# The last two rounds of a mixture of experts: a gated sum on VectorE instead of identity products on TensorE

## The reference, cut to what matters

```python
x  = layer_norm(ALPHA * x + g1 * mix, ln1_g, ln1_b)
h2 = x * (1.0 + sc2) + sh2
y2 = sum over e of comb[t, e] * (silu(h2 @ w_gate[e]) * (h2 @ w_up[e])) @ w_down[e]   # 16 experts
x  = layer_norm(ALPHA * x + g2 * y2, ln2_g, ln2_b)
```

## Time and profile before

| | us |
|---|---|
| median of 3 runs | 480.96 (479.89 to 482.44) |
| the profiled execution | 481.61 |
| its span, first to last instruction | 479.8 |
| TensorE busy | 433.2 (90%) |
| VectorE busy | 244.1 (51%) |
| ScalarE busy | 120.8 (25%) |
| TensorE's mean granted clock | 0.975 of full |

### The profile page before, as it was taken

How to read it: one execution, slowest core, us unless ns; L and a number is a source line. 1 busy time by engine, 2 the same in 40 slices (tenths; PEclk the granted TensorE clock), 3 DMA queues, 4 the chain that set the end, 5 groups by cost and what they waited for, 6 DMA issues and landing times.

```text
span 479.8 us, 6399 instructions
## 1 busy us (share of the span) xinstructions
PE 433.2 (90%) x2352; PEld 229.2 (48%) x2352; DVE 244.1 (51%) x457; ACT 120.8 (25%) x229; POOL 39.9 (8%) x41
## 2 busy tenths in 40 slices
PE   0878999999999988899999999999999999899850
PEld 0434555555444443784554355554455554355220
DVE  4562725737864687971132353344554445333666
ACT  3300186285311032360120011121111111021143
POOL 2000043054000000390000000000000000000000
PEclk9999999999999995999999999999999999999995
DMA  8999994408999883808999999999999999999303
GB/s 300 387 387 381 305 387 146 161 0 198 386 387 404 333 290 104 308 2 314 376 396 397 370 359 395 396 391 392 397 394 391 393 396 394 392 392 404 127 2 132
DMA packets 65363, 149.50 MB, mean 312 GB/s; under 512 B 3624, under 2 KB 4504, under 8 KB 64936
## 3 DMA queue, kind: packets, MB, share of 16 engines
q1 hardware_dynamic: 63776, 143.33, 80.7%
q10 hardware_dynamic: 1384, 5.48, 2.9%
q0 software_dynamic: 160, 0.10, 0.5%
HBM read 147.30 MB, written 1.60 MB: 310 GB/s over the span
## 4 chain that ended last, share of the span: by engine, by line
PE 74%; DMA 9%; DVE 5%; issue 4%; ACT 4%; SPq 3%; DVEq 0%; ACTq 0%
PE PS L1746 19%; PE PS L1541 11%; PE PS L1623 9%; PE PS L1786 8%; PE PS L1752 6%; DMA ring<-in_w_ada 5%; PE PS L1820 4%; DMA ring<-in_ex_w_gate 4%; PE PS L1703 3%; SPq L379 3%; PE PS L1479 3%; PE PS L1524 2%; PE PS L1793 1%; PE PS L1828 1%; PE PS L1766 1%
## 5 line engine op out<-in xcount | busy, mean ns | idle before, releaser
L1746 PE MATMUL PS<-ring,xs 128*64 128x256 f32 x896 | 102.9, 382 | 1.3 <-DMA ring<-in_ex_w_gate 1.2
L1746 PEld LDWEIGHTS PS<-ring,xs 128*64 128x64 f32 x896 | 61.9, 137 | 37.7 <-issue 9.1
L1541 PE MATMUL PS<-hT,ring 128*128 128x388 f32 x192 | 65.3, 491 | 2.9 <-DMA ring<-in_w_in 2.1
L1786 PE MATMUL PS<-ring,hTs 128*64 128x512 f32 x224 | 51.1, 598 | 2.2 <-ACT hTs L675 1.4
L1541 PEld LDWEIGHTS PS<-hT,ring 128*128 128x128 f32 x192 | 36.1, 190 | 30.4 <-DMA ring<-in_w_in 2.4
L1288 DVE SCALAR_TENSOR_TENSOR y<-PS,comb,y 128x1024 f32<-128x1024 f32 x39 | 49.8, 1277 | 0.3 <-PE PS L1828 0.3
L1786 PEld LDWEIGHTS PS<-ring,hTs 128*64 128x64 f32 x224 | 14.8, 136 | 31.0 <-issue 30.9
L1274 DVE TENSOR_TENSOR yl<-PS,yh 128x512 fp32r<-128x512 f32 x12 | 8.3, 692 | 41.0 <-ACT yh L693 41.0
L1752 PE MATMUL PS<-ring,xs 128*128 128x512 f32 x64 | 28.0, 592 | 0.0
L693 ACT CAST yh<-PS 128x512 fp32r<-128x512 f32 x12 | 7.0, 587 | 81.3 <-PE PS L1786 62.9
L1479 PE MATMUL PS<-ring,cond 128*32 128x512 f32 x192 | 24.9, 656 | 2.1 <-DMA ring<-in_w_ada 2.1
(11 more groups left out here) (270 smaller groups left out, 554.8 us busy)
## 6 DMA issues: line engine op xcount, KB each, us to landing
ring<-in_ex_w_gate SPq DMA_DIRECT2D x16, 2048.0 KB, 13.4
ring<-in_ex_w_up SPq DMA_DIRECT2D x16, 2048.0 KB, 13.5
ring<-in_ex_w_down SPq DMA_DIRECT2D x16, 2048.0 KB, 14.2
ring<-in_w_ada SPq DMA_DIRECT2D x12, 2048.0 KB, 16.1
ring<-in_w_in SPq DMA_DIRECT2D x3, 2048.0 KB, 20.4
ring<-in_w_out SPq DMA_DIRECT2D x2, 2048.0 KB, 18.4
rows<-row_scratch ACTq DMA_DIRECT2D x3, 1024.0 KB, 7.6
xn<-in_x_sample SPq DMA_DIRECT2D x2, 512.0 KB, 6.7
```

Of the source, the lines that this page charges most:

```text
L1541: mm = pe.matmul(PS[:, w % 4, 0:W], wt[:, k, (w % 4) * P:(w % 4 + 1) * P], hT[:, k, :], start=(k == 0), stop=(k == KD - 1))
L1746: mm = pe.matmul(PS[HALF * h:HALF * (h + 1), j, 0:FE // 2], x[:, k, 0:HALF], w[:, k, h * (FE // 2):(h + 1) * (FE // 2)], start=(k == 0), s ...
L1786: mm = pe.matmul(PS[HALF * h:HALF * (h + 1), yb, :], x, w[:, f, h * 512:(h + 1) * 512], start=(f == 0), stop=(f == KF - 1))
```

## The change

- `add_sum` is gone. TensorE's end is now combine(14, 0), combine(14, 1), combine(15, 0), combine(15, 1), combine(14, 2), combine(15, 2), and every combine of expert 14 starts its banks anew.
- A new step `gated(i)` on VectorE multiplies `y12[:, i, :]` (the sum of the first 14 experts) by `g2` and adds `ALPHA * xn`, in place, once `gather(13, i)` is done. `gated(0)` stands before `hidden(15)`, `gated(1)` after `gather(13, 1)`, `gated(2)` after `choose(15)` and before `y_low(15)`.
- `z(i)` multiplies the banks by `g2` into a new tile `ztmp` (in the ring slot of expert 15's gate weights), then adds `y12[:, i, :]`; this second instruction also gives the row's sum by `accum_out`, so ScalarE's pass over the row for the sum (L751) is gone.
- `choose` is cut in two: `row_weights(e)` (the look-up) and `choose(e)` (`selT`). `row_weights(14)` and `choose(14)` move from round 14 to the end of round 13, after gather(12, 2); `row_weights(15)` and gather(13, 2) move before `y_low(14)`; `choose(15)` stands after `y_low(14)`.
- ScalarE runs a square root on a scratch column after `hid_out(14)`, and `hid_out(15)` moves before `y_out(14)`. Its order in the tail is moments(0), root, moments(1), root, moments(2), root.

```diff
+        ztmp = at("ztmp", base + (3 * LAST - 1) % SLOTS * RB, [P, NT, D])
...
-                hid_out(e)
+                if e < LAST:
+                    hid_out(e)
+                if e == LAST - 1:
+                    act.activation(small[:, 4:5], cst[:, 0:1], ACT.Sqrt)
+                    hid_out(LAST)
...
                 act.wait_ge(s["z_done"], i + 1)
                 need(act, "mom_sq", i)
-                act.activation(gsum[:, :], y12[:, i, :], ACT.Copy, accum_out=stat[:, i, 0:1]).then_inc(s["mom_sum"], 1)
-                act.wait_ge(s["mom_sum"], i + 1)
                 act.activation(stat[:, i, 1:2], stat[:, i, 0:1], ACT.Copy, scale=-1.0 / D).then_inc(s["mom_mean"], 1)
...
-                moments(0)
-                moments(1)
-                root(2 * NT)
-                moments(2)
-                root(2 * NT + 1)
-                root(2 * NT + 2)
+                for i in range(NT):
+                    moments(i)
+                    root(2 * NT + i)
...
+            def gated(i):
+
+                m = y12[:, i, :]
                 if i == 0:
                     dve.wait_ge(s["g2_sb"], 4)
+                dve.wait_ge(s["acc_done"], NT * (LAST - 2) + i + 1)
+                link(dve.tensor_tensor(m, m, g2r[:, 1 if i else 0, :], ALU.mult))
+                dve.scalar_tensor_tensor(out=m, in0=xn[:, i, :], scalar=ALPHA, in1=m, op0=ALU.mult, op1=ALU.add)\
+                    .then_inc(s["gated"], 1)
+
+            def z(i):
+
+                m, b = y12[:, i, :], c_banks(LAST, i)
                 dve.wait_ge(s["p_ps"], i + 1)
-                link(dve.tensor_tensor(m, PS[:, b:b + 2, :].rearrange("p a n -> p (a n)"), g2r[:, 1 if i else 0, :],
-                                       ALU.mult))
-                dve.scalar_tensor_tensor(out=m, in0=xn[:, i, :], scalar=ALPHA, in1=m, op0=ALU.mult, op1=ALU.add)\
-                    .then_inc(s["z_done"], 1)
+                link(dve.tensor_tensor(ztmp[:, i, :], PS[:, b:b + 2, :].rearrange("p a n -> p (a n)"),
+                                       g2r[:, 1 if i else 0, :], ALU.mult))
+                dve.wait_ge(s["gated"], i + 1)
+                dve.scalar_tensor_tensor(out=m, in0=ztmp[:, i, :], scalar=1.0, in1=m, op0=ALU.mult, op1=ALU.add,
+                                         accum_out=stat[:, i, 0:1]).then_inc(s["z_done"], 1)
...
                 if e:
                     gather(e - 1, 0)
+                if e == LAST - 1:
+                    gated(0)
                 hidden(e + 1)
-                choose(e)
+                if e < LAST - 1:
+                    choose(e)
                 if e:
                     gather(e - 1, 1)
+                if e == LAST - 1:
+                    gated(1)
+                    row_weights(LAST)
+                    gather(e - 1, 2)
                 y_low(e)
-                if e == LAST - 1:
-                    choose(LAST)
-                if e:
+                if 0 < e < LAST - 1:
                     gather(e - 1, 2)
+                if e == LAST - 2:
+                    row_weights(LAST - 1)
+                    choose(LAST - 1)
+
+            choose(LAST)
+            gated(2)
             y_low(LAST)
...
             for i in range(NT - 1):
                 combine(LAST - 1, i)
-                add_sum(i)
             for i in range(NT - 1):
                 combine(LAST, i)
-            add_sum(NT - 1)
             combine(LAST - 1, NT - 1)
             combine(LAST, NT - 1)
```

More of the change, by code:

```diff
@@ L250, in build @@
             "gelu_done yr_done maps_ps maps_sb fold_done z_ps z_sb f_ps yf_sb row_ps row_sb mix_ps x1n "
-            "g1_out g1_in mod2_out sc2_in sh2_in "
+            "gated g1_out g1_in mod2_out sc2_in sh2_in "
             "x1_done h2_done mod2_done h2hi h2lo h2T_ps h2T_sb lg_ps assign_done rank_ps route_done "
@@ L258, in build @@
             "g2_ps g2_sb fin_done wrow_ps wrow_sb wsum_a wsum_b p_ps z_done "
-            "out_done var_done root_done mom_sum mom_mean mom_sq").split()}
+            "out_done var_done root_done mom_mean mom_sq").split()}
         pos_in = [sem(f"pos_in{i}") for i in range(NT - 1)]
@@ L1232, in choose, with rows_of, row_weights @@
                 need(dve, "c_ps", NT * (e - 1))
+                def rows_of(q):
+                    dve.tensor_scalar(seltmp[:, :], Prow[:, 0, :], io[:, q, e:e + 1], None, ALU.is_equal)\
+                        .then_inc(s["selA2"], 1)
+                    dve.wait_ge(s["selA2"], e + 1)
+                    dve.scalar_tensor_tensor(out=selT[e % 2][:, :], in0=Prow[:, 1, :], scalar=io[:, q, e:e + 1],
+                                             in1=seltmp[:, :], op0=ALU.is_equal, op1=ALU.add).then_inc(s["selT_done"], 1)
+                fork(dve, counts[e], lambda: rows_of(0), lambda: rows_of(1))
+            def row_weights(e):
                 if e == LAST - 1:
                     dve.wait_ge(s["wrow_sb"], 2)
+                need(dve, "selT_done", e)
                 def weights_of(q):
@@ L1245, in weights_of @@
                     dve.wait_ge(s["wsum_b"], e - LAST + 2)
[L1247 to L1256, removed]
+                fork(dve, counts[e], lambda: weights_of(0), lambda: weights_of(1))
             def y_low(e):
@@ L1289, in gather @@
                                              op0=ALU.mult, op1=ALU.add).then_inc(s["acc_done"], 1)
+            def gated(i):
+                m = y12[:, i, :]
+                if i == 0:
+                    dve.wait_ge(s["g2_sb"], 4)
+                dve.wait_ge(s["acc_done"], NT * (LAST - 2) + i + 1)
+                link(dve.tensor_tensor(m, m, g2r[:, 1 if i else 0, :], ALU.mult))
+                dve.scalar_tensor_tensor(out=m, in0=xn[:, i, :], scalar=ALPHA, in1=m, op0=ALU.mult, op1=ALU.add)\
+                    .then_inc(s["gated"], 1)
             def z(i):
                 m, b = y12[:, i, :], c_banks(LAST, i)
-                if i == 0:
-                    dve.wait_ge(s["g2_sb"], 4)
                 dve.wait_ge(s["p_ps"], i + 1)
-                link(dve.tensor_tensor(m, PS[:, b:b + 2, :].rearrange("p a n -> p (a n)"), g2r[:, 1 if i else 0, :],
-                                       ALU.mult))
-                dve.scalar_tensor_tensor(out=m, in0=xn[:, i, :], scalar=ALPHA, in1=m, op0=ALU.mult, op1=ALU.add)\
-                    .then_inc(s["z_done"], 1)
+                link(dve.tensor_tensor(ztmp[:, i, :], PS[:, b:b + 2, :].rearrange("p a n -> p (a n)"),
[3 more added lines that the diff above has]
+                                         accum_out=stat[:, i, 0:1]).then_inc(s["z_done"], 1)
             silu(0)
@@ L1808, in combine @@
                     pe.wait_ge(s["acc_done"], NT * (LAST - 1))
-                first = e < LAST - 1 or (e == LAST - 1 and i < NT - 1)
+                first = e < LAST
                 stop = e != LAST - 1
@@ L1832, in combine @@
                 fork(pe, counts[e], few, many)
[L1834 to L1842, removed]
             def weight_row(q):
```

## The result

The changed kernel's median is 475.53 us (475.22 to 476.33, 4 runs) against 481.14 us of the kernel before (479.89 to 482.44, 4 runs): a ratio of 0.9887, 95% interval 0.9866 to 0.9908. The forecast was 475.7.

What follows compares the result with a forecast made beforehand. TensorE was taken to bound the end from 449.83 us, then VectorE's queue after the change. First z 3.55 plus tail 1.78 gave 5.33 us gained, 475.6 as a median, stated as 475.7; range 474.3 to 477.4.

Steps and rivals of the forecast that it cites:

- The bound passes to VectorE's queue: After project_out(15), combine(15, 0) waits for y_low(15) on VectorE; TensorE alone would give 4.7 us, 1.1 of them lost.
- rival 4: Gated passes between 440 and 454 us run at half rate, 2.29 us each, adding 6.25 us: median 481.9; chance 0.05.
- The first z: End of the expert loop: z(0) starts at 455.87 instead of 459.42 us, 3.55 us gained.
- Round 13 ... I count nothing: Moved row_weights(14) and choose(14) take 2.51 us, within VectorE's 2.58 us wait ahead of silu(15); at worst 0.3 us late.
- Rival 1: VectorE's queue of eleven steps and three branches runs 0.15 us later for each, losing 1.65 us: 477.3; chance 0.11.
- The tail: From first z to VectorE's last end: 15.57 us instead of 17.35, 1.78 gained, VectorE never waiting.
- Rival 3: The accumulator halves the rate of z's addition, 3.2 us over three steps in the tail: 478.9; chance 0.04.
- The table load: Moved early, it hides in ScalarE's idle 8.70 us ahead of 448.37; its worth is near nothing.
- Rival 2: The table load is placed again inside the tail's branch, costing 0 to 0.3 us: 475.7 to 476.0; chance 0.02.
- TensorE's clock: Around project_out(15) and combine(15, 0): TensorE's new pauses are about 1.1 us each, no longer than the earlier 1.35.

Runs made afterwards that it cites:

- e1: Kernel before with only the accumulator in z and ScalarE's sum pass gone: first z 24.96, tail 15.25, median 479.32 us.
- e12: Changed kernel with identity products back and no gated passes; new orders, accumulator and early table load kept: first z 24.19, tail 15.25, median 478.55 us.
- e3: Changed kernel without the early square root, so the table load is back in the tail: tail 15.26, median 476.02 us.
- e10: Changed kernel timed and profiled again, as it is: first z 22.19, tail 15.26, median 476.17 us.
- e2: Changed kernel without the accumulator, sum pass back on ScalarE: first z 22.18, tail 16.47, median 477.47 us.
- e4: Changed kernel with hid_out(15) behind y_out(14) again: first z 22.18, tail 15.26, median 476.58 us.
- e8: Changed kernel with turn(15) ahead of combine(13, 2) on TensorE: first z 22.45, tail 15.26, median 476.08 us.
- e5: Changed kernel with all three gated steps moved behind y_low(15): first z 27.33, tail 15.24, median 481.06 us.
- e7: Changed kernel with gated(2)'s second pass moved behind y_low(15): first z 21.28, tail 15.26, median 475.92 us.
- e6: Changed kernel with expert 14's look-up and choice in one branch, weight wait moved from the branch to y_low: first z 21.60, median 476.93 us.
- e9: Changed kernel with one branch for expert 14, gated(2) split around y_low(15), and turn(15) ahead of combine(13, 2): first z 21.51, median 475.11 us.
- e11: Changed kernel with one branch for expert 14 and gated(2) split around y_low(15), turn(15) in its old place: first z 22.57, median 475.77 us.

## Why the prediction was right, and where its sizes were off

The terms, from runs that add one part after another to the kernel before (sum of first z and tail, us):

| step | forecast | measured | from |
|---|---|---|---|
| accumulator instead of ScalarE's pass | 1.78 | 2.09 | before to e1: 42.30 to 40.21 |
| orders on VectorE and ScalarE, early table load | within 3.55 | 0.77 | e1 to e12: 40.21 to 39.44 |
| gated passes instead of identity products | within 3.55 | 1.95 | e12 to after: 39.44 to 37.49 |
| early table load alone | near 0 | 0.00 | e3 to e10: 37.45 and 37.45 |

What a part is worth depends on what stands already: the accumulator is 2.09 us on the kernel before and 1.2 us on the changed one (e2).

*The bound passes to VectorE's queue.* Right: e4 and e8 move TensorE's path by 0.5 and 0.75 us with no gain or loss of that size, e5 and e7 move VectorE's and the first z follows. That the passes run at 1.22 us each with DMAs under way was right too: gated(0)'s multiply took 1.23 us with the DMA engines busy throughout, gated(2)'s 1.22 us with none. That settles rival 4, whose price was off besides: by its own 0.94 ns an element half rate is 0.96 us more a pass, not 1.07, and six times 1.07 is 6.42, not 6.25. What the passes can cost by their place alone is shown by e5.

```profile
440.85:442.11 1.26, 1.26 (x14) 0.65 (x10) 1.23 (x2) 0.00 (x0) 0.00 (x0) 1.00 1.00 397
...
451.92:453.17 1.25, 1.25 (x10) 0.67 (x8) 1.22 (x2) 0.68 (x1) 0.00 (x0) 1.00 0.00 0
```

*The first z, 2.70 instead of 3.55.* The step that was mis-sized is "Round 13 ... I count nothing". I priced look-up and choice together at the 2.51 us that they take inside one branch, but the change puts them into two. Behind a wait at the end of the look-up's branch VectorE stood idle: 0.52 us in round 13, and 0.30 behind the second look-up (e6). Another 0.25 ahead of silu(15) came on top, for which no run shows the cause. I looked for cover behind silu(15) on TensorE's side, and found the 2 us; but gated(0) had used up VectorE's own, down to the last 0.01 us. So silu(15), 0.66 us late (5.12 instead of 4.46), came out as 0.56 us at gather(13, 1) (9.57 instead of 9.01); the look-up of expert 15 adds 0.27 (0.47 instead of 0.20 behind its last addition), and these make up 0.83 of the 0.85 us. With one branch 0.65 us come back (e6). Rival 1 came nearest to it, with what a branch costs where nothing hides it, though it is a branch that ends on a wait.

*The tail, 2.11 instead of 1.78.* The accumulator's read-out, priced at 0.10 us in each of three steps, is hidden: the steps from z to z were 2.41 and 2.47 us instead of 2.50 and 2.57. Rival 3 is settled: 1.22 us at 1024 elements from two float32 SBUF sources, with the accumulator as without it. So the trace does not bear out, for this instruction, what the Trainium skill says of half throughput ("Vector Engine (DVE) Microarchitecture Reference", section "Points that are easy to get wrong").

*The table load.* Right, and for the reason given (e3). Rival 2 was the case in which it stays; the load ran at 439.24 in the changed kernel, in ScalarE's idle time.

*TensorE's clock.* Wrong in a detail that cost little here: I counted pauses of about 1.1 us, it was 2.02, and the clock fell to half while combine(15, 0) ran. Its second half took 0.46 us instead of 0.39, and the first z came 1.95 us behind the start of y_low(15) instead of 1.88 (e2, e10). The combines behind it took 0.63 us instead of 0.40; nobody waited for them.

```profile
456.00:457.00 1.00, 1.00 (x8) 0.80 (x6) 0.74 (x1) 0.00 (x0) 0.00 (x0) 0.50 0.00 0
```

The median of 475.5 agrees with 475.7 better than the terms deserve: two errors of 0.85 and 0.33 us had opposite signs, and the first four runs were 0.6 us below the six that came later.

## What to carry to other kernels

When work moves to an engine that is half idle, its price is set by its place in that engine's queue: the same six passes cost 0.8 us spread over the queue and 5 us more ahead of the first consumer. Rebuild the queue from start-to-start steps, and price a branch by its own rows: a wait that closed a branch's body kept the next instruction from overlapping. And shorten the queue that bounds before the path beside it; a faster TensorE gained nothing here and lost a little by its longer pause, and in the profiles with VectorE's queue shortened twice (e9, e11) a late landing of weights moved the first z.

## What the runs showed of the hardware

- A wait at the end of a branch's body left VectorE idle for 0.30 and 0.52 us ahead of the next instruction. Without it the next pass started 0.07 to 0.08 us behind the start of a 0.16 us addition (e6); with it inside the branch, 0.20 us behind (kernel before).
- An addition of 128x1024 from two float32 SBUF sources took 1.22 us with an accumulator, as without one; the read-out of 0.08 us started together with the next instruction (changed kernel, tail).
- TensorE's granted clock, ahead of combine(15, 0): where it had paused for 1.14 to 1.82 us (e3 to e7, e9 to e11) it stayed at 1.00; where it had paused for 2.02, 2.03 and 2.78 us (after, e2, e8) it fell to half (1.2 GHz) within the next microsecond. The length of the pause does not settle it everywhere: in an earlier stage, behind the same pause of 1.22 us, the clock was 0.50 in the next microsecond in one profile of the changed kernel and 1.00 in the other (first line: first profile; second: e10).

```profile
179.62:180.62 1.00, 1.00 (x5) 1.00 (x6) 1.00 (x2) 0.31 (x1) 0.00 (x0) 0.50 1.03 385
...
179.78:180.78 1.00, 1.00 (x8) 0.85 (x8) 1.00 (x2) 0.30 (x1) 0.00 (x0) 1.00 1.04 397
```

- The landing of the last down weights varies from run to run with the same work up to there: those of expert 14 took 18.8 us from issue to landing in the changed kernel's first profile and 20.4 in e10 and e11. project_out(14) waited 0.77 and 0.78 us for them in e10 and e11, project_out(15) 0.59 us for its own in e9; neither waited for weights in the first profile.
